# Two transformer blocks on one core: other squares, another order of centring, and a later bank ahead of the first mixer

## What is computed

```python
def layer_norm(x, g, b):
    xf = x.astype(jnp.float32)
    mu = jnp.mean(xf, axis=-1, keepdims=True)
    var = jnp.mean(jnp.square(xf - mu), axis=-1, keepdims=True)
    y = (xf - mu) * lax.rsqrt(var + LN_EPS) * g.astype(jnp.float32) + b.astype(jnp.float32)
    return y.astype(x.dtype)
...
        x = layer_norm(DEEPNORM_ALPHA * x + mix, ln_g[l, 0], ln_b[l, 0])
        x = layer_norm(DEEPNORM_ALPHA * x + swiglu(x, ffn_w_in[l], ffn_w_out[l]), ln_g[l, 1], ln_b[l, 1])
...
def rmsnorm(x, g):
    xf = x.astype(jnp.float32)
    y = xf * lax.rsqrt(jnp.mean(xf * xf, axis=-1, keepdims=True) + EPS)
    return (y * g.astype(jnp.float32)).astype(x.dtype)
...
    h = jnp.concatenate([meta, x], axis=1)
...
        h = h + hybrid_mixer(rmsnorm(h, norm_mix_g[l]), w_in[l], ...)
```

## Time and profile before

| | |
|---|---|
| median of 3 runs | 2631.39 us (2630.84 to 2632.81) |
| the profiled execution: its own time | 2633.11 us |
| its span, from the first to the last instruction | 2631.3 us |
| PE busy | 2594.8 us, 99% of the span |
| DVE busy | 1360.1 us, 52% |
| ACT busy | 1038.6 us, 39% |
| mean granted TensorE clock | 0.998 of full speed |

### The profile page before, as it was taken

How to read it: one execution, slowest core, us unless ns; L and a number is a source line. 1 busy time by engine, 2 the same in 40 slices (tenths; PEclk the granted TensorE clock), 3 DMA queues, 4 the chain that set the end, 5 groups by cost and what they waited for, 6 DMA issues and landing times.

```text
span 2631.3 us, 42709 instructions
## 1 busy us (share of the span) xinstructions
PE 2594.8 (99%) x18898; PEld 2320.8 (88%) x18898; DVE 1360.1 (52%) x2200; ACT 1038.6 (39%) x1702; POOL 40.1 (2%) x90
## 2 busy tenths in 40 slices
PE   9999999999999999999999999999999999999998
PEld 7777888888887788888899899999999989999998
DVE  6766533324657643333567446555336754655523
ACT  4554422213545432221455344443224534544421
POOL 0000000000100000000000000000000000000000
PEclk9999999999999999999999999999999999999999
DMA  5222222222322122222231222222223113222222
GB/s 189 89 61 69 95 91 90 90 102 77 110 64 79 65 96 96 96 90 94 90 105 50 73 96 91 89 89 93 89 94 120 66 58 105 91 87 97 93 89 77
DMA packets 40010, 235.76 MB, mean 90 GB/s; under 512 B 5536, under 2 KB 7840, under 8 KB 17936
## 3 DMA queue, kind: packets, MB, share of 16 engines
q1 hardware_dynamic: 35056, 214.45, 24.0%
q0 software_dynamic: 4048, 17.00, 2.0%
q10 hardware_dynamic: 720, 1.57, 0.2%
HBM read 222.38 MB, written 6.42 MB: 87 GB/s over the span
## 4 chain that ended last, share of the span: by engine, by line
PE 94%; DVE 4%; ACT 1%; DMA 1%; issue 0%; SPq 0%; DVEq 0%; ACTq 0%
PE P L552 77%; PE P L666 3%; PE P L644 3%; PE P L559 2%; PE P L678 1%; DVE WL L1839 1%; PE P L914 1%; PE P L1027 1%; PE P L935 1%; PE P L724 1%; PE P L692 1%; ACT WH L1274 0%; PE P L1077 0%; DVE X L1982 0%; DMA X<-in_xT 0%; PE P L1079 0%
## 5 line engine op out<-in xcount | busy, mean ns | idle before, releaser
L552 PE MATMUL P<-XH,WL 128*128 128x264 f32 (+3 forms) x3080 | 844.4, 323 | 17.5 <-DVE XL L1999 6.0
L552 PE MATMUL P<-XL,WH 128*128 128x264 f32 (+3 forms) x3080 | 823.1, 316 | 0.0
L552 PE MATMUL P<-XH,WH 128*128 128x264 f32 (+3 forms) x3080 | 820.4, 315 | 0.0
L1839 DVE TENSOR_TENSOR WL<-raw,WH 128x1024 fp32r<-128x1024 f32 (+2 forms) x405 | 483.1, 1196 | 530.9 <-ACT WH L1274 530.3
L1274 ACT ACTIVATE WH<-raw 128x1024 fp32r<-128x1024 f32 (+2 forms) x405 | 417.5, 1035 | 592.1 <-PE P L552 587.0
L552 PEld LDWEIGHTS P<-XH,WL 128*128 128x128 f32 x3080 | 520.3, 188 | 67.4 <-DVE XL L1999 8.0
L552 PEld LDWEIGHTS P<-XH,WH 128*128 128x128 f32 x3080 | 518.9, 189 | 38.0
L552 PEld LDWEIGHTS P<-XL,WH 128*128 128x128 f32 x3080 | 518.8, 188 | 36.5
L2534 DVE SCALAR_TENSOR_TENSOR tmp<-P,PP,tmp 128x527 f32<-128x527 f32 (+1 forms) x88 | 66.8, 759 | 195.2 <-ACT tmp L1784 195.2
L552 PE MATMUL P<-GHH,WL 128*128 128x264 f32 (+1 forms) x704 | 149.1, 283 | 0.0
L552 PE MATMUL P<-GHL,WH 128*128 128x264 f32 (+1 forms) x704 | 148.9, 282 | 0.0
(11 more groups left out here) (347 smaller groups left out, 3413.2 us busy)
## 6 DMA issues: line engine op xcount, KB each, us to landing
raw<-in_wts SPq DMA_DIRECT2D x167, 1024.0 KB, 4.9
raw<-in_wts SPq DMA_DIRECT2D x32, 896.0 KB, 4.6
spill<-X POOLq DMA_DIRECT2D x2, 2112.0 KB, 9.3
X<-spill POOLq DMA_DIRECT2D x16, 264.0 KB, 3.0
qswap<-qraw SPq DMA_DIRECT2D x44, 64.0 KB, 2.0
tab<-in_tR POOLq DMA_DIRECT2D x2, 1056.0 KB, 5.3
tmp<-in_biasT POOLq DMA_DIRECT2D x16, 128.0 KB, 3.0
tmp<-in_biasT POOLq DMA_DIRECT2D x16, 112.0 KB, 2.7
```

The lines of the kernel that those rows point to most:

```text
L552: ins = nc.tensor.matmul(P[:, a:a + x1 - x0], wb[:, s, 128 * k:128 * k + 128], xb[:, kx, x0 - c0:x1 - c0], start=start and i == 0, stop=st ...
L1839: nc.vector.tensor_tensor(WL[:, u % NS, 0:length(u)], raw[:, u // 2 % RAW, a:a + length(u)], WH[:, u % NS, 0:length(u)].bitcast(F), ALU.su ...
```

## The change

Norm s = 3 is changed in five ways.

- `square_again` no longer squares X. It squares `ln_g * q + ln_b`, with q the quotient that `normal` leaves, and takes ln_g and ln_b as per-partition scale and bias operands of the same ScalarE instruction; it waits for `normal` in place of `result`. The 16 meta tokens are squared by three small instructions of their own.
- `normal` and `result` write in place in X, all eight `normal` of a half first and then all eight `result`, each of which waits for the square that reads the same chunk.
- The eight `centre` of the second half move from ahead of `rms_half` of the first half to inside it, two behind each of chunks 3 to 6. Their squares on ScalarE move to behind `feed` of chunks 4 to 7, and the weights' high part for unit u+2 (`highs(top + 3)`) to behind all of them.
- On TensorE the variance sums of the second half move from ahead of and behind chunks 1 and 2 of phase 0 to behind chunks 5, 6 and 7 of phase 0 and behind chunk 0 of phase 1; its sums of squares all stand behind phase 1.
- `early_two` takes bank 4 when its third unit begins.

```diff
@@ -574,7 +574,7 @@
-            def early_halves(u, seg, ver, one_bank, between):
+            def early_halves(u, seg, ver, one_bank, between, third=()):
@@ -585,6 +585,7 @@
                 pe.wait_ge(*at("wlo", u + 2))
+                take(*third)
                 for k in range(8):
@@ -601,8 +602,8 @@
             def early_two(u, ver, between):
-                take(0, 1, 2, 3, 4, 5)
-                early_halves(u, lambda n, hf: pair_of(n, ver - 1)[hf], ver, False, between)
+                take(0, 1, 2, 3, 5)
+                early_halves(u, lambda n, hf: pair_of(n, ver - 1)[hf], ver, False, between, (4,))
@@ -837,14 +838,15 @@
                     sums(0, 4, 5, 6, 7)
-                    var(1, 0, 1, 2, 3)
...
                     if s == 3:
-                        if phase == 0 and k in (1, 2):
-                            var(1, 2 * k + 2, 2 * k + 3)
-                        elif phase == 1 and k % 4 == 3:
-                            sums(1, *range(k - 3, k + 1))
+                        if phase == 0 and k >= 5:
+                            var(1, 2 * k - 10, 2 * k - 9)
+                        elif phase == 1 and k == 0:
+                            var(1, 6, 7)
+                        elif phase == 1 and k == 7:
+                            sums(1, *range(8))
                     elif phase == 0:
@@ -1392,23 +1394,18 @@
                     for m in range(8):
-                        square_again(s, m, 0)
-                        if m == 4:
-                            highs(top + 2)
-                    for m in range(4):
-                        square(m, 1)
+                        square_again(l, s, m, 0)
+                    highs(top + 2)
                     root_again(s, 0)
...
                         feed(s, m, 0)
-                        if m < 2:
-                            square(2 * m + 4, 1)
-                            square(2 * m + 5, 1)
-                        elif m == 3:
-                            highs(top + 3)
-                        elif m == 4:
-                            root(1)
+                        if m >= 4:
+                            square(2 * m - 8, 1)
+                            square(2 * m - 7, 1)
+                    highs(top + 3)
+                    root(1)
                     for m in range(8):
-                        square_again(s, m, 1)
+                        square_again(l, s, m, 1)
                     root_again(s, 1)
@@ -1428,14 +1425,19 @@
-            def square_again(s, m, hf):
-                a, b = tokens(s)[hf]
-                act.wait_ge(*at("xf", s, m, hf))
-                if not hf:
-                    act.wait_ge(meta_loaded, 16)
+            def square_again(l, s, m, hf):
...
+                a, b = HV[hf]
                 if m >= 6:
                     act.wait_ge(*at("ms", s, m - 6, hf))
-                nc.scalar.activation(SQ[:, m % 6, a:b], X[:, m, a:b], ACT.Square).then_inc(*act.up("xsq", s, m, hf))
+                if not hf and m in (0, 6, 7):
+                    n = 6 if m == 0 else 1
+                    act.wait_ge(meta_loaded, 16)
+                    nc.scalar.activation(SQ[:, m % 6:m % 6 + n, 0:META], X[:, m:m + n, 0:META], ACT.Square).then_inc(*act.up("msq", s, m))
+                act.wait_ge(*at("nrm", s, m, hf))
+                k = 16 * l + 8 + m
+                nc.scalar.activation(SQ[:, m % 6, a:b], X[:, m, a:b], ACT.Square, bias=par("ln_b", k), scale=par("ln_g", k)
+                                     ).then_inc(*act.up("xsq", s, m, hf))
@@ -1985,11 +1987,11 @@
                     dve.wait_ge(*at("rsl", s, hf))
-                    if m >= 4:
-                        dve.wait_ge(*(at("xf", s, m - 4, hf) if s == 3 else at("xl", ver, m - 4, hf)))
                     if s == 3:
-                        nc.vector.tensor_tensor(tmp[m % 4][:, a:b], X[:, m, a:b], rstd[:, a:b], ALU.mult).then_inc(*dve.up("nrm", s, m, hf))
+                        nc.vector.tensor_tensor(X[:, m, a:b], X[:, m, a:b], rstd[:, a:b], ALU.mult).then_inc(*dve.up("nrm", s, m, hf))
                     else:
+                        if m >= 4:
+                            dve.wait_ge(*at("xl", ver, m - 4, hf))
                         nc.vector.scalar_tensor_tensor(tmp[m % 4][:, a:b], X[:, m, a:b], par("ln_g", p0 + m), rstd[:, a:b], ALU.mult, ALU.mult
@@ -2002,8 +2004,8 @@
                     k = p0 + m
-                    dve.wait_ge(*at("nrm", s, m, hf))
-                    nc.vector.tensor_scalar(X[:, m, a:b], tmp[m % 4][:, a:b], par("ln_g", k), par("ln_b", k), ALU.mult, ALU.add
+                    dve.wait_ge(*at("xsq", s, m, hf))
+                    nc.vector.tensor_scalar(X[:, m, a:b], X[:, m, a:b], par("ln_g", k), par("ln_b", k), ALU.mult, ALU.add
                                             ).then_inc(*dve.up("xf", s, m, hf))
@@ -2015,16 +2017,16 @@
                         normal(m, 0)
+                    res(7, 1)
+                    for m in range(8):
                         result(m, 0)
-                        if m == 4:
-                            res(7, 1)
                     lows(top + 2)
-                    centre(1, *range(8))
                     g0 = pc["nmix"]
-                    rms_half(s, g0, 0)
+                    rms_half(s, g0, 0, lambda m: centre(1, 2 * m - 6, 2 * m - 5) if 3 <= m < 7 else None)
                     lows(top + 3)
...
                         normal(m, 1)
+                    for m in range(8):
                         result(m, 1)
@@ -2052,6 +2054,8 @@
                         dve.wait_ge(*at("rstd", s, hf))
+                        if s == 3:
+                            dve.wait_ge(*at("xf", s, m, hf))
                         if m >= 4 and s < 7:
@@ -2061,8 +2065,8 @@
                                                 ).then_inc(*dve.up("xl", s + 1, m - 2, hf))
-                    if m == 3 and beside:
-                        beside()
+                    if beside:
+                        beside(m)
@@ -2252,10 +2256,11 @@
-                def beside():
-                    if last == 1:
-                        lows(top + 2)
-                    res(7, 1)
+                def beside(m):
+                    if m == 3:
+                        if last == 1:
+                            lows(top + 2)
+                        res(7, 1)
...
                     res(m, 0)
```

## The result

The change makes the kernel slower by 3.7 us: the median of 21 runs is 2636.16 us against 2632.43 us for 21 runs of the kernel before, a ratio of 1.0016 with a 95% interval of 1.0010 to 1.0022. That is a difference clear of the measurement and, by the bound of 0.2%, the case called "same". Its profiled execution took 2636.71 us, with a span of 2634.9 us against 2631.3, 3.6 us more.

The account below looks back on a forecast made before the run. TensorE, busy 2594.8 of 2631.3 us, bounds the kernel, so its second-half start decides: variance 5.8 us later less 2.4 us shorter from `normal` gives +3.4, added to 2631.39 makes 2634.8 us; range 2631.0 to 2637.8 us.

Parts of the forecast that it names:

- the case called "same": Whole kernel: a difference of less than 0.2%, which is 5.3 us, counts as no change; chance 0.80.
- First half: On TensorE, sums of squares start at 1284.92 and phase 0 at 1292.3, 1.6 us earlier than before.
- Centres: Eight `centre` inside `rms_half` add 2.7 us; VectorE needs 1.43 us a chunk for 0.73 us of TensorE matmuls.
- gaps of 0.7 us between chunks: Sign of being right: TensorE idles 0.7 us between the chunks of phase 0.
- Late variance: Second half's variance root comes late, so VectorE starts `normal` at 1307.43 against 1301.65, 5.8 us later.
- Squares: ScalarE's squares with two operands take 0.61 us, 0.50 apart; the operand rule costs 0.15 us here, not 3.0.
- From `normal` to the second half: From VectorE's first second-half `normal` to TensorE's second half: 8.03 us against 10.43 before, 2.4 us shorter.
- The clock rival: Clock falls in the gap ahead of phase 0 and stays low over chunks 5 and 6: +6.6, 2638.0 us; chance 0.13.
- the main forecast: Second half starts at 1315.46 against 1312.08: +3.4 us, median 2634.8 us; chance 0.60.
- signs of being wrong: Granted clock under 1 between 1292 and 1304, squares much over 0.61 us, or second-half `normal` before 1304.
- The cover up to chunk 4: In phase 0, a half-clock chunk takes 1.32 us, inside VectorE's 1.43, so a low clock is hidden up to chunk 4.
- The last gap: Ahead of the second half the gap stays 2.8 us; rival without clock fall there: +1.9, 2633.3 us, chance 0.15.

Follow-up runs that it names:

- first gap filled: Changed kernel plus five sums of a constant into a free bank between the first half's last sum of squares and phase 0; stretch 31.48 us, median 2636.27 us.
- Copy early: Changed kernel, but the weight copy of unit u+2 goes back to behind the fourth feed; stretch 30.09 us, median 2634.61 us, ratio 1.0009.
- variance first: Changed kernel, but the variance sums of chunks 6 and 7 stand at the end of phase 0; stretch 30.37 us, median 2634.98 us, ratio 1.0010.
- centre ahead: Changed kernel, but all eight second-half `centre` stand ahead of the first half's `rms_half`; stretch 31.42 us, median 2636.03 us, ratio 1.0016.
- quotient alone: Changed kernel keeping only quotient squares, in-place `normal` and `result` eight by eight, and the later `take`, in the old order; stretch 26.89 us, median 2631.55 us.

## Why the prediction was right

The forecast was +3.4 us and 2634.8 us on the median of three runs; measured are +3.7 us, and 2636.16 us against a median that itself came out at 2632.43 with more runs. So the absolute time was 1.4 us too low, 1.0 of it from its base of three runs; the difference is what was forecast well. In the profiles the second half starts 3.60 us later (3.38 forecast), and the 0.2 us too much was there already at `normal`. Step by step:

- **First half.** Sums at 1285.01 (1284.9 forecast), phase 0 at 1292.52 (1292.3); 1.4 us sooner than before, where 1.6 was forecast. The new trace runs 0.05 us late from 1280.6 on; the rest is in the sums, the last of which ends at 1289.72 and not 1289.52.
- **Centres.** A chunk every 1.43 us, as worked out; chunk 5's XL let its matmuls start at 1298.88 (1298.8). The gaps of 0.7 us between chunks were not seen: at half clock the first chunks follow without one, and ahead of chunks 4 and 5 it is 0.26 and 0.44. At full clock, with the first gap filled, it is 0.39 to 0.43, since the profile lets a chunk's last matmul last 0.28 us and the forecast counted 0.12.
- **Late variance.** The wait for WL is 1.10 us (1.1); `normal` at 1307.64 (1307.43). 6.0 us later than before, against 5.8. Copy early and variance first take 1.39 and 1.11 us away, each alone, which shows two of the queues in it. The centres' place is worth 1.57 when the clock is held up (31.48 to 29.91). These three make 4.07 us of the 4.59 that the new order costs, but they were not tried together, and the squares behind feeds 4 to 7 were not tried alone; how the rest divides is not shown.
- **Squares.** 0.50 us apart, 4.10 us for eight (4.11), 0.60 each (0.61). Without the operands the eight take 1.2 us less, and each 0.424 on the mean instead of 0.595, so two operands add 0.17 us. The Trainium skill (ScalarE: Activation LUTs, What ACT_TABLE_LOAD costs) has about 93 ns for each pointer operand; the trace roughly agrees for two of them, with 85 ns each. That its price would be paid only to 0.15 us was the prediction's reading; 0.23 was measured.
- **From `normal` to the second half** 8.04 us (8.03).
- **The clock rival.** The clock did fall in the first gap, which the main forecast did not count on: a granted clock under 1 between 1292 and 1304 was one of its signs of being wrong, and it was 0.57 from 1292 to 1296. It was back near 1296.0, in the midst of chunk 2. The cover up to chunk 4 was worked out ahead; that the spell ended in time was not, and in that the number was lucky. The claim that half clock is hidden there is shown by the filled gap (31.48 both times). In centre ahead, with a chunk every 0.75 us, the same fall cost 1.5 us. The rule of the Trainium skill (TensorE: Matmul & The Clock Gate, A second HAM failure mode) that small idle times between groups of matmuls can let the clock swing, beside which this rival stood, is not shown by this stretch: the clock came back within the half-idle phase 0, and both falls followed one long gap each. Elsewhere one profile is in line with it: in that of quotient alone the clock fell near 905.9 us behind idle times of only 0.94 and 0.61 us (rows at the end).
- **The last gap** of 2.71 us cost the same in both, so the chance that it would give 1.5 us back was not taken up by the profiled execution.

What is not settled: why the clock falls behind one gap of 2.7 us and not behind the next, and once behind much shorter ones. Medians hold a mixture of both.

## What to carry to other kernels

Before an instruction is moved off the path of one result, list what is queued behind its new place on that engine, and follow each of these to who waits. Here a weight copy behind squares that wait for sums, and sums behind matmuls that wait for that copy's low part, cost more (`normal` 6.0 us later) than the quicker squares gave back behind them (2.4 us).

A latency that cannot be shortened (sum, Ln, Exp, first products: 2.7 us) is paid only where nothing is left to do: keep a piece of independent work of that length for it. In the five profiles here in which no gap over 0.6 us was left ahead of the second half, the clock also stayed up behind it. And a faster chain brings its full gain only when the other engines' order is made for it.

## What the runs showed of the hardware

- Square with a per-partition scale and bias takes 0.60 us for 264 columns (mean of eight) and follows another by 0.50; without them 0.42 and 0.35 (paced by VectorE).
- In this stretch a granted clock at half (1.2 GHz) followed 13 of 15 gaps of 2.70 to 3.94 us, and none of 1.67 us and less. It lasted some three us as a rule, and in one profile some six, with TensorE busy all the time:

```profile
1313.46:1319.00 5.54, 5.54 (x25) 5.54 (x26) 4.38 (x12) 2.18 (x6) 1.10 (x3) 0.50 0.69 293
```

- A long gap is not needed. In the profile of quotient alone TensorE was idle for 0.94 and 0.61 us, with twelve matmuls between, and from 905.9 to about 909 the clock was at half: matmuls started 0.21 to 0.22 us apart in place of 0.11 to 0.12. The kernel before has the same two gaps there (0.95 and 0.62 us), and its clock stayed at 1.00.

```profile
903.32 0.36 PE L552 MATMUL P<-XH,WL 128*128 128x248 f32 x1 [0.94 <-DVE XL L2005]
905.59 0.47 PE L552 MATMUL P<-XH,WL 128*128 128x248 f32 x1 [0.61 <-DVE XL L2005]
```

- With five sums of a constant (2.39 us of otherwise idle TensorE) ahead of the second half, the gap was 0.48 us and the clock stayed at 1.00 behind it, in one profile each of the two kernels.
